# Four blocks of queries in the reverse order, in the attention of a six-layer kernel

## What is computed

```python
c = jnp.cumsum(log_f, axis=1).transpose(0, 2, 1)
q_blocks = q.reshape(B, FOX_HEADS, n_blk, Q_BLOCK, FOX_HEAD_DIM).transpose(2, 0, 1, 3, 4)

def one_block(args):
    q_b, c_b, start = args
    logits = jnp.einsum('bhqd,bhkd->bhqk', q_b, k) * scale
    logits = logits + c_b[..., :, None] - c[..., None, :]
    mask = key_pos[None, :] <= q_pos[:, None]
    p = jax.nn.softmax(jnp.where(mask, logits, -jnp.inf), axis=-1)
    return jnp.einsum('bhqk,bhkd->bhqd', p, v)
```

## Time and profile before

| | |
|---|---|
| median of three runs | 3925.47 us |
| the profiled execution's own time | 3926.31 us |
| its span in the profile | 3924.5 us |
| TensorE busy with matmuls | 3649.6 us, 93% |
| VectorE busy | 2065.8 us, 53% |
| ScalarE busy | 1080.3 us, 28% |
| GpSimd busy | 1096.8 us, 28% |
| mean granted clock of TensorE | 0.959 |

### The profile page before, as it was taken

One profiled execution on the slowest core, in us unless ns is written; L12 is line 12 of the kernel. 1 busy time (PEld: TensorE's weight loads), 2 busy tenths in 40 slices (PEclk: granted clock), 3 DMA queues, 4 the chain that ended last, 5 costly groups with the idle time before them and its releaser, 6 DMA issues. The chain is left out here.

```text
span 3924.5 us, 44371 instructions
## 1 busy us (share of the span) xinstructions
PE 3649.6 (93%) x16819; PEld 2845.9 (73%) x16819; DVE 2065.8 (53%) x2631; ACT 1080.3 (28%) x1480; POOL 1096.8 (28%) x835
## 2 busy tenths in 40 slices
PE   7999999878999979999899999987899999789999
PEld 6767888657788858887667888753688877257887
DVE  4556555894544475454555545655533346554334
ACT  4542221032212122212542221333321223332221
POOL 0635542700645236340544543012100000130000
PEclk9999999889999989999999999987999998899999
DMA  3215443033444334432214443200133321013332
GB/s 105 65 49 135 122 136 105 27 71 93 129 131 135 87 93 135 130 106 83 54 46 123 130 131 104 75 13 22 57 97 103 88 80 45 22 44 86 91 96 81
DMA packets 554319, 346.08 MB, mean 88 GB/s; under 512 B 33270, under 2 KB 535420, under 8 KB 554172
## 3 DMA queue, kind: packets, MB, share of 16 engines
q1 hardware_dynamic: 540348, 293.79, 26.6%
q0 software_dynamic: 13824, 50.34, 4.4%
HBM read 341.01 MB, written 3.08 MB: 88 GB/s over the span
## 5 line engine op out<-in xcount | busy, mean ns | idle before, releaser
L1273 PE MATMUL ps<-h_hi,w_hi 128*128 128x512 f32 x2880 | 1144.6, 397 | 41.6 <-DVE w_lo L1235 14.6
L1274 PE MATMUL ps<-h_lo,w_hi 128*128 128x512 f32 x2880 | 1127.4, 391 | 0.0
L1275 PE MATMUL ps<-h_hi,w_lo 128*128 128x512 f32 x2880 | 1126.2, 391 | 0.0
L1235 DVE TENSOR_TENSOR w_lo<-w,w_hi 128x2048 fp32r<-128x2048 f32 (+2 forms) x294 | 664.3, 2260 | 133.8 <-ACT w_hi L1228 131.7
L1228 ACT ACTIVATE w_hi<-w 128x2048 fp32r<-128x2048 f32 (+2 forms) x294 | 507.0, 1725 | 711.9 <-PE ps L1275 638.1
L1273 PEld LDWEIGHTS ps<-h_hi,w_hi 128*128 128x128 f32 x2880 | 545.1, 189 | 161.9 <-issue 36.1
L1275 PEld LDWEIGHTS ps<-h_hi,w_lo 128*128 128x128 f32 x2880 | 543.9, 189 | 115.2
L1274 PEld LDWEIGHTS ps<-h_lo,w_hi 128*128 128x128 f32 x2880 | 544.8, 189 | 107.9 <-issue 0.5
L1364 DVE TENSOR_TENSOR sg<-sg,ps 128x512 f32<-128x512 f32 x132 | 90.8, 688 | 719.2 <-ACT sg L1349 719.2
L1273 PE MATMUL ps<-a_hi,w_hi 128*128 128x512 f32 x1056 | 411.9, 390 | 0.0
L1275 PE MATMUL ps<-a_hi,w_lo 128*128 128x512 f32 x1056 | 411.0, 389 | 0.0
(11 more groups left out here) (471 smaller groups left out, 3971.6 us busy)
## 6 DMA issues: line engine op xcount, KB each, us to landing
w<-in_ffn_w_gate_up SPq DMA_DIRECT2D x176, 512.0 KB
w<-in_w_ada POOLq DMA_DIRECT2D x96, 512.0 KB, 6.9
w<-in_ffn_w_down SPq DMA_DIRECT2D x64, 704.0 KB
w<-in_w_gate_up SPq DMA_DIRECT2D x88, 512.0 KB
w<-in_w_down SPq DMA_DIRECT2D x32, 704.0 KB
w<-in_fox_w_in SPq DMA_DIRECT2D x32, 512.0 KB
w<-in_w_in SPq DMA_DIRECT2D x14, 1024.0 KB
w<-in_fox_w_in SPq DMA_DIRECT2D x8, 1024.0 KB
```

The costliest lines, as they stand in the source:

```text
L1235: last = nc.vector.tensor_tensor(lo, raw, hi.bitcast(F32), ALU.subtract)
L1273: nc.tensor.matmul(out, hi, a[0][:, k, :], start=k == 0, stop=False)
L1274: nc.tensor.matmul(out, hi, a[1][:, k, :], start=False, stop=False)
L1275: return nc.tensor.matmul(out, lo, a[0][:, k, :], start=False, stop=k == kt - 1)
```

## The change

Step `t` of a head now works on the block of queries `3 - t`: the block with 512 keys comes first and that with 128 last, in all four attention stages. Logits, maxima, exponentials, scalings and transposes of a step all go with their block. Semaphores, banks and the order of the steps stay, and so do the places of projections, staging, copies and products with V. The buffers of the probabilities are chosen by block, so each block still has its own; the statistics are chosen by step.

```diff
     def logits(self, e, s, t):
         m, mm, i = self.m, self.m.nc.tensor.matmul, ST * s + t
-        n = (t + 1) * P
+        b = self.block(t)
+        n = (b + 1) * P
...
-        out, at = m.ps[:, 2 + t % 2, 0:n], slice(t * P, n)
+        out, at = m.ps[:, 2 + t % 2, 0:n], slice(b * P, n)
...
+    @staticmethod
+    def block(t):
+
+        return ST - 1 - t
+
     def turn(self, e, s, t):
         m, nc, i = self.m, self.m.nc, ST * s + t
+        q = self.block(t)
         e.wait_ge(m.sem["p_scaled"], m.at("p_scaled", i + 1))
...
-        for b in range(t + 1):
-            part, at = self.PT_AT[b][0], self.PT_AT[b][1] + (t - b) * P
-            last = nc.tensor.transpose(m.ps[:, 4 + part, at:at + P], self.pb[s % 2][t][:, b * P:(b + 1) * P], m.c("ident"))
+        for b in range(q + 1):
+            part, at = self.PT_AT[b][0], self.PT_AT[b][1] + (q - b) * P
+            last = nc.tensor.transpose(m.ps[:, 4 + part, at:at + P], self.pb[s % 2][q][:, b * P:(b + 1) * P], m.c("ident"))
...
-                nc.scalar.activation(self.pb[s % 2][t], m.ps[:, 2 + t % 2, 0:(t + 1) * P], ACT.Exp, bias=self.stat(self.nm, s, t),
+                b = self.block(t)
+                nc.scalar.activation(self.pb[s % 2][b], m.ps[:, 2 + t % 2, 0:(b + 1) * P], ACT.Exp, bias=self.stat(self.nm, s, t),
...
-            nc.gpsimd.tensor_scalar(self.pb[s % 2][t], self.pb[s % 2][t], self.stat(self.ri, s, t), None, ALU.mult).then_inc(m.sem["p_scaled"], 1)
+            p = self.pb[s % 2][self.block(t)]
+            nc.gpsimd.tensor_scalar(p, p, self.stat(self.ri, s, t), None, ALU.mult).then_inc(m.sem["p_scaled"], 1)
...
-                nc.vector.tensor_reduce(self.stat(self.nm, s, t), m.ps[:, 2 + t % 2, 0:(t + 1) * P], AX.X, ALU.max, negate=True).then_inc(m.sem["max_ready"], 1)
+                nc.vector.tensor_reduce(self.stat(self.nm, s, t), m.ps[:, 2 + t % 2, 0:(self.block(t) + 1) * P], AX.X, ALU.max, negate=True).then_inc(m.sem["max_ready"], 1)
```

More of the change, by code:

```diff
@@ L1989, in logits @@
             e.wait_ge(m.sem["exp_ready"], m.at("exp_ready", i - 1))
-        n = (t + 1) * P
+        b = self.block(t)
+        n = (b + 1) * P
         bank = m.ps[:, 2 + t % 2, :]
-        mm(bank[:, 0:n], self.up.q(m, s)[:, t * P:n], self.up.k(m, s)[:, 0:n], start=True, stop=False)
-        mm(bank[:, t * P:n], m.identb[:], m.futureb[:], start=False, stop=True).then_inc(m.sem["logits_ready"], 1)
+        mm(bank[:, 0:n], self.up.q(m, s)[:, b * P:n], self.up.k(m, s)[:, 0:n], start=True, stop=False)
+        mm(bank[:, b * P:n], m.identb[:], m.futureb[:], start=False, stop=True).then_inc(m.sem["logits_ready"], 1)
 class SplitProject(Split):
```

## The result

The changed kernel takes 3938.97 us, median of 6 runs (3938.49 to 3944.56), against 3924.76 us (3918.07 to 3926.23, 6 runs) for the kernel before beside it: ratio 1.0043, 95% interval 1.0030 to 1.0056. That is slower by more than 0.2%, where no change was forecast, and above the range. The profiled execution took 3939.04 us, its span 3937.2 us, at a mean clock of 0.961.

What follows compares the result with a forecast made beforehand. It saw Fox stages bound by TensorE, other engines nearly hidden, and TensorE waiting in every latent head. Terms +1.2 (latent pairs), -3.6 (latent starts), +1.0 (Fox stages) sum to -1.4 us: 3924.0 us predicted, range 3917 to 3932.

Steps and rivals of the forecast that it cites:

- TensorE goes on 1.15 after the copies begin: Duration step for a head's transposes: TensorE resumes 1.15 us after VectorE's copies of the turned probabilities begin.
- what is late now is the maximum of the 512 block: Latent pair: copies stand behind that maximum in VectorE's queue, so the copy wait grows slightly more than the bank wait shrinks.
- A latent pair: Two latent heads, first logits to product with V: +0.20 us on 10.30, +1.2 us over three pairs in two stages.
- The bound from both sides: Latent pair: -0.33 us if only the smaller bank wait counts, +0.80 if only the later transposes do.
- A Fox pair: Fox stages: staging 0.11 us sooner, copies 0.30 later, net +0.19; six such places in a stage, +1.1 us.
- The last Fox pair: End of each Fox stage, without projections: 7.55 us after its transposes instead of 8.15, so -0.6 us.
- A latent stage's start: First heads of a latent stage at the lower clock: -1.8 us per stage, -3.6 us for two, bounds 0 and -3.
- the early rise of the clock: Latent stage's start: no gap in work after 2713.1, so the clock may rise earlier, counted as -0.5 us.
- The first rival: Latent stages: clock falls as copy waits grow, 2.4 us a head, half of twelve heads +14, 3938 us; chance 0.10.
- The rule cited from the Trainium skill: Latent stages: short TensorE idle times at PSUM bank changes can make the clock swing; would give the 3938 us result.
- signs of being right: Latent pairs 10.5 us, ScalarE wait near 0.5, VectorE copy waits 1.2 to 1.4, third head 1 sooner, Fox pairs 0.2 longer.
- signs of being wrong: Granted clock of the latent stretch under 0.95, GpSimd waits before transposes, or Fox pairs moving by over 0.5 us.

Runs made afterwards that it cites:

- e1: Changed kernel with ScalarE's copy moved ahead of the exponential of a head's first block, VectorE's copies left in place: 3926.82 us, ratio 1.0006.
- f3: Changed kernel again, unchanged, for a second profile and more runs: 3940.27 us, ratio 1.0043.
- e4: Kernel before with the reverse block order in the two Fox stages alone: 3926.08 us, ratio 1.0012.
- e2: Changed kernel with ScalarE's copy ahead of a head's first exponential and VectorE's two copies ahead of its first maximum: 3899.63 us, ratio 0.9944.
- g2: Changed kernel with all three copies ahead of the first maximum and exponential, run a second time: 3899.74 us, ratio 0.9950.
- g1: Changed kernel with block order 128, 512, 384, 256 keys, no copy moved: 3907.01 us, ratio 0.9967.

## Why the prediction was wrong

**The step that failed** is "TensorE goes on 1.15 after the copies begin". It was measured on VectorE's copies, the only ones on which a wait was recorded, and it was carried over to an order in which another engine's copy ends last. ScalarE's copy was never placed: it stands behind the first exponential, in the lines that the change rearranges. With 128 keys ahead it left no wait, level with VectorE's in an even head (3473.71 and 3473.72); with 512 it ends 0.32 us after VectorE's. The working "what is late now is the maximum of the 512 block" stopped one engine short: maximum, exponential, then copy.

**A latent pair, +0.20 forecast, +0.98 measured.** The bank wait went from 0.87 to 0.49, 0.54 forecast: right. The copies begin 1.90 after the first logits, 1.80 forecast, and VectorE's alone would let the transposes begin at 3.04 (e1), 2.95 forecast: 0.09 a head. ScalarE's copy makes it 3.36, another 0.32 a head. The sum is 0.20 - 0.05 + 2 x 0.09 + 2 x 0.32 = 0.97, against 0.98 measured. The bound from both sides, -0.33 to +0.80, did not hold the value, because both ends were drawn from VectorE's rows.

**A Fox pair, +0.19 forecast, +0.38 measured.** The VectorE part was right (+0.20 in e1), and ScalarE's copy adds 0.18. The sum over five steady gaps is +1.9 us a stage, not +1.1.

**The last Fox pair, -0.6 forecast, +1.4 and +1.6 measured** in the two stages. Two waits for ScalarE's copy stand there without projections (TensorE's timeline, first Fox stage, after; for the earlier trace rows):

```profile
242.02 0.96 PE L1777 MATMUL ps<-consts,misc 128*128 128x128 f32 x7 [2.27 <-ACT sg L1870]
...
247.44 1.73 PE L1777 MATMUL ps<-consts,misc 128*128 128x128 f32 x7 [1.70 <-ACT sg L1870]
```

Before, the same two waits were 1.57 and 0.64 us, and the granted clock from 248 to 252 us is now 0.71. In the second Fox stage of f3 and of e4 the last two gaps are 19.56 us together (12.91 + 6.65 in e4) against 22.0 here (13.73 + 8.29), and 20.6 before. So the sign of this term depends on where the clock falls, which the forecast did not allow for.

**A latent stage's start, -1.8 forecast.** TensorE's timeline, first latent stage, after, the first logits of three heads:

```profile
2717.09 2.04 PE L2002 MATMUL ps<-arena 96*128 96x512 f32 x2 [13.02 <-PEq L2973]
...
2725.33 2.07 PE L2002 MATMUL ps<-arena 96*128 96x512 f32 x2 [0.47 <-ACT arena L1882]
...
2732.57 1.12 PE L2002 MATMUL ps<-arena 96*128 96x512 f32 x2 [0.26 <-ACT arena L1882]
```

The second head starts 8.24 us after the first (8.55 before: -0.31, -0.35 forecast), the third 15.48 us (16.81 before, from 2704.90 to the 2721.71 of the earlier trace rows: -1.33). In the second latent stage the third head gained 0.82 us. The mechanism was right; the early rise of the clock that I had counted was not seen, and the two stages gave -2.1, not -3.6.

**The clock.** The first rival said that the clock falls in the latent stages, in half of 12 heads at 2.4 us, and it gives the measured 3938 us by luck. It is right in part: the clock does fall after some of the new waits. Of the twelve waits of 1.4 us in the first profile eleven were followed by transposes at the upper clock (0.96 us for seven) and one, before 3462.47, by transposes at the lower (1.73 us); in the second profile it was three of twelve. With the last pairs that makes two low stretches in the first profile and five in the second (latent stages of 61.95 and 64.74 us), mostly at some 1.6 us each (one in the second profile took 3.0). Before, there was one, in the last pair of the first latent stage (8.83 for 6.66); the prediction, which saw no fall in a latent stage, had overlooked it. The net is one to four falls at 1.6 us, not six at 2.4; the copy waits are the larger part.

Each of these falls begins behind a wait for a copy, and in e2, g2 and g1, where those waits are short or gone, the last gap of every latent stage is the short one, at most 6.66 us, although the two waits at a stage's end (1.87 and 1.11 us) are the same there. That the waits cause the falls is therefore likely, but it was not tried by itself, and the number of falls does not follow the length of the wait: e1, with waits of 1.1 us, has six, more than either profile of the changed kernel. The prediction's reading of the old waits gave no ground either: it called 1.33 us nearer to the 1.05 that the clock survived than to the 1.57 before a fall, but it lies 0.28 from the one and 0.24 from the other. The rule cited from the Trainium skill ("TensorE: Matmul & The Clock Gate", section "A second HAM failure mode: psum-queue depth-cycling"), of a clock that swings where TensorE is idle for a short time at each change of PSUM bank, is not borne out for the steady pairs of the first profile, which stayed at 1.00 through a wait of 1.4 us in each head; the falls that came are single ones.

**Signs.** Of the prediction's signs of being right, the 0.5 us bank wait, the earlier third head and the longer Fox pairs (by 0.38 us, not 0.2) came. The wait of 1.2 to 1.4 us before the transposes came too, at 1.41, but for the other engine. Its signs of being wrong did not come in the first profile: the granted clock of the steady latent stretch is 1.00, no wait for GpSimd stands before the transposes, and a steady Fox pair moved by under 0.5 us. None of them looked at which engine's copy is the last.

**What stays open.** The medians differ by 14.2 and 16.8 us, the attention stages of the profiles by 10.8 and 13.1. The 3 to 4 us between have no place that repeats. Taken as measured, the forecast's own terms give 5.9 us for six latent pairs, -2.1 for the starts, 3.8 for ten steady Fox gaps and 3.0 for the last Fox pairs: +10.6 us, near the 10.8 of the four stages; the falls of the clock, one more in net, and small differences at the stages' starts make up the rest.

## What to carry to other kernels

When a step's first operation grows longer, list everything that stands behind it on every engine, and take for each consumer the last of its producers, not the one that the old trace names: a producer that was just early enough (here, in an even head, by 0.01 us) leaves no wait in the profile. An order of work and the place of the copies in it are one choice. Against the kernel before, descending order costs 0.43% with the copies behind the first block and gains 0.50 to 0.56% with all copies ahead; the copies ahead in the old order gain 0.16%; descending order with VectorE's copies alone ahead costs 0.98%. The version without any move of a copy is the place of the long block: as the second one, where its matmuls cover the copies, it gains 0.33%, and it differs from the changed kernel in one line.

## What the runs showed of the hardware

The first state-space stage took 66.0 or 66.1 us in some profiles and 73.3 us in others with the same instructions, by how long the granted clock stayed low while TensorE was busy all the time (28.00 of 28.00 us at a clock of 0.63, against 27.71 at 0.90). Over 29 runs the kernel before ranged from 3914.99 to 3928.47 us, 0.34%, and its two profiled runs (3926.31 and 3928.88 us) lay near its upper end. A difference of 0.2% between two single profiles of this kernel says little; the length of one pair, which repeats to 0.04 us as long as the clock does not fall in it, says much. The clock can fall to its lower level behind a wait of 1.1 us (e1, 3480.96), and wait after wait of 1.4 us can pass without a fall (11 of 12 in the first profile of the changed kernel).
